# Narrow TensorE products placed between wide ones, and the transposes of the probabilities spread through the work behind them

## The reference

```python
logits = (q @ k) * scale; logits = where(kpos <= qpos, logits, -inf)      # MLA; MoBA adds a bias
p = softmax(logits); out = p @ v
# layer 1
z = (q @ k) * scale
log_1m = where(strict, log_sigmoid(-z), 0.0)
acc = cumsum(log_1m, reverse) - log_1m
w = where(strict, exp(log_sigmoid(z) + acc), 0.0); out = w @ v
```

## Time and profile before

| | us |
|---|---|
| median of 3 runs (lowest to highest) | 1331.95 (1331.87 to 1332.46) |
| the profiled execution | 1332.39 |
| its span | 1330.6 |
| PE busy, share | 1291.9, 97% |
| DVE, ACT, POOL busy | 734.3, 554.5, 260.1 |

### The profile page before, as it was taken

How to read it: one execution, slowest core, us unless ns; L and a number is a source line. 1 busy time by engine, 2 the same in 40 slices (tenths; PEclk the granted TensorE clock), 3 DMA queues, 4 the chain that set the end, 5 groups by cost and what they waited for, 6 DMA issues and landing times.

```text
span 1330.6 us, 17696 instructions
## 1 busy us (share of the span) xinstructions
PE 1291.9 (97%) x6599; PEld 1093.1 (82%) x6599; DVE 734.3 (55%) x998; ACT 554.5 (42%) x885; POOL 260.1 (20%) x205
## 2 busy tenths in 40 slices
PE   6989999999999999999999999999999999999997
PEld 5677788898888888888888888887988888888886
DVE  4777654538644454422288787776574455443223
ACT  5456665546322223322354555454453322223112
POOL 1532200025211111100051111320441111110002
PEclk9989999999999999999999999999999999999999
DMA  5412222122333333333222111311223333332331
GB/s 163 132 43 71 65 72 72 48 79 81 111 95 95 99 101 96 87 101 96 83 79 65 48 48 52 90 48 47 81 81 110 95 95 95 95 112 93 95 96 63
DMA packets 190503, 112.34 MB, mean 84 GB/s; under 512 B 13696, under 2 KB 184773, under 8 KB 190446
## 3 DMA queue, kind: packets, MB, share of 16 engines
q1 hardware_dynamic: 188636, 106.81, 27.6%
q0 software_dynamic: 640, 2.10, 0.5%
q10 hardware_dynamic: 1170, 2.66, 0.5%
HBM read 109.43 MB, written 4.74 MB: 86 GB/s over the span
## 4 chain that ended last, share of the span: by engine, by line
PE 85%; DVE 8%; ACT 3%; issue 2%; POOL 1%; DMA 0%; POOLq 0%; ACTq 0%; SPq 0%; DVEq 0%
PE banks L433 26%; PE banks L435 25%; PE banks L434 25%; PE banks L1712 3%; DVE w_lo L428 1%; PE banks L1742 1%; PE banks L1630 1%; PE banks L1459 1%; DVE logits L1421 1%; PE banks L482 1%; DVE tf L702 1%; ACT logits L1432 1%; DVE probsT_lo L1471 1%; POOL stick_lo L1729 0%; DVE u_lo L712 0%
## 5 line engine op out<-in xcount | busy, mean ns | idle before, releaser
L428 DVE TENSOR_TENSOR w_lo<-w_raw,w_hi 128x1024 fp32r<-128x1024 f32 (+3 forms) x200 | 288.0, 1443 | 264.9 <-ACT w_hi L421 264.7
L433 PE MATMUL banks<-u_hi,w_hi 128*128 128x512 f32 (+1 forms) x1112 | 424.9, 382 | 5.8 <-DVE w_lo L428 4.3
L435 PE MATMUL banks<-u_hi,w_lo 128*128 128x512 f32 (+1 forms) x1112 | 419.1, 377 | 0.0
L434 PE MATMUL banks<-u_lo,w_hi 128*128 128x512 f32 (+1 forms) x1112 | 418.9, 377 | 0.0
L421 ACT ACTIVATE w_hi<-w_raw 128x1024 fp32r<-128x1024 f32 (+3 forms) x200 | 206.0, 1031 | 277.0 <-PE banks L435 277.0
L433 PEld LDWEIGHTS banks<-u_hi,w_hi 128*128 128x128 f32 x1112 | 210.2, 189 | 45.7 <-issue 4.9
L435 PEld LDWEIGHTS banks<-u_hi,w_lo 128*128 128x128 f32 x1112 | 210.1, 189 | 38.8
L434 PEld LDWEIGHTS banks<-u_lo,w_hi 128*128 128x128 f32 x1112 | 210.3, 189 | 37.8 <-issue 1.0
L905 POOL TENSOR_TENSOR up<-up,gate 128x512 f32<-128x512 f32 x44 | 71.8, 1632 | 375.2 <-DVE up L931 358.4
L886 ACT ACTIVATE gate<-gate 128x512 f32<-128x512 f32 x44 | 27.8, 632 | 202.3 <-DVE gate L927 202.3
L1729 POOL TENSOR_TENSOR stick_lo<-softplus,stick_hi 128x1280 fp32r<-128x1280 f32 x14 | 44.1, 3164 | 156.9 <-DVE stick_hi L1725 156.9
(11 more groups left out here) (256 smaller groups left out, 1987.5 us busy)
## 6 DMA issues: line engine op xcount, KB each, us to landing
w_raw<-in_ffn_w_gate_up_dram SPq DMA_DIRECT2D x88, 512.0 KB, 3.6
w_raw<-in_ffn_w_down_dram SPq DMA_DIRECT2D x30, 512.0 KB, 3.6
w_raw<-in_sb_w_qkv_dram SPq DMA_DIRECT2D x24, 512.0 KB, 3.6
w_raw<-in_ab_w_in_dram SPq DMA_DIRECT2D x17, 512.0 KB, 3.6
w_raw<-in_ffn_w_down_dram SPq DMA_DIRECT2D x16, 448.0 KB, 3.6
w_raw<-in_ab_w_out_dram SPq DMA_DIRECT2D x8, 512.0 KB, 3.8
w_raw<-in_sb_w_out_dram SPq DMA_DIRECT2D x8, 512.0 KB, 4.5
bias_by_distance<-bias_rows ACTq DMA_DIRECT2D x1, 2560.0 KB
```

What stands on the lines that cost most here:

```text
L428: dve.tensor_tensor(wl[:, c.slot, 0:w], raw[:, c.slot, 0:w], wh[:, c.slot, 0:w].bitcast(F32), ALU.subtract).then_inc(w_lo, 1)
L433: nc.tensor.matmul(o, lh, rh, start=start, stop=False, skip_group_check=True)
L434: nc.tensor.matmul(o, lh, rl, start=False, stop=False, skip_group_check=True)
L435: return nc.tensor.matmul(o, ll, rh, start=False, stop=stop, skip_group_check=True)
```

## The change

1. `mm3` takes a generator `narrow` and pulls one matmul from it after each of its three; `project`, `item_pe` and `scores_pe` hand it through (the four transposes of a "vt" slot don't use it).
2. `probs_pe` becomes such a generator. A step issues the first transpose, and the other nine go one by one behind the matmuls of slot a where that is a projection, then behind those of the first two score tiles of head `hh + 2`; what is left follows the scores.
3. `scores_pe`: the narrow tile's three matmuls go between those of the 384-wide tile. `values`: the last block's three go between those of the first. `c_pe`: the eight narrow ones go singly behind wide ones. `sb_pv_pe`: the two narrow ones go between and behind the two 512-wide ones. `z_pair_pe`: for each of three terms the two heads' 256-wide blocks, then their two narrow ones (before: six narrow ones in a row, then six 256-wide ones).
4. A tensor of 128 bytes a partition is put ahead of the latent tensors, which moves them by that much.

```diff
+            sb(at0, "latent_line_pad", [P, 32])
...
-        def mm3(o, lh, ll, rh, rl, start, stop):
+        def mm3(o, lh, ll, rh, rl, start, stop, narrow=iter(())):
             nc.tensor.matmul(o, lh, rh, start=start, stop=False, skip_group_check=True)
+            next(narrow, None)
             nc.tensor.matmul(o, lh, rl, start=False, stop=False, skip_group_check=True)
+            next(narrow, None)
-            return nc.tensor.matmul(o, ll, rh, start=False, stop=stop, skip_group_check=True)
+            mm = nc.tensor.matmul(o, ll, rh, start=False, stop=stop, skip_group_check=True)
+            next(narrow, None)
+            return mm
...
-            for i in (3, 1, 2, 0):
+            def first_tile():
+                o = SC[:, ROW_AT[0]:ROW_AT[0] + P]
+                for lq, rk in ((qh, kh), (qh, kl), (ql, kh)):
+                    mm = nc.tensor.matmul(o, lq[:, 0:P], rk[:, 0:P], start=False, stop=lq is ql, skip_group_check=True)
+                    if lq is ql:
+                        mm.then_inc(sc_done, 1)
+                    yield
+
+            for i in (3, 1, 2):
                 mm = mm3(SC[:, at:at + w], qh[:, q], ql[:, q], kh[:, 0:w], kl[:, 0:w],
-                         start=(i != 0), stop=True)
+                         start=True, stop=True, narrow=first_tile() if i == 2 else narrow)
...
-            mm.then_inc(pt_done, 1)
+                    if j == TT - 1:
+                        mm.then_inc(pt_done, 1)
+                    yield
...
+            def last_block():
+                o, at = out_bank[:, P * (TT - 1):T], COL_AT[TT - 1] + at0
+                for lv, rx in ((v[0], xh), (v[0], xl), (v[1], xh)):
+                    nc.tensor.matmul(o, lv[:, buf, TT - 1, cols], rx[:, at:at + P], start=False, stop=False,
+                                     skip_group_check=True)
+                    yield
...
-            for j in (0, 1, 3, 2):
+            for blocks in ((0,), (1,), (2, 3)):
                 for n, (lhs, rhs) in enumerate(Z_TERMS):
-                    for e in range(2):
-                        z_block(par, e, j, lhs, rhs, j != 3 and n == 0)
+                    for j in blocks:
+                        for e in range(2):
+                            z_block(par, e, j, lhs, rhs, j != 3 and n == 0)
...
+            def last_blocks():
+                for j in range(TT):
+                    for n in (nsh, nsl):
+                        yield block(j, TT - 1, n)
+            narrow = last_blocks()
+            for j in range(TT - 1):
+                for jj in range(j, TT - 1):
+                    for n in (nsh, nsl):
+                        mm = block(j, jj, n)
+                        if (j, jj) != (0, 0) and (j, jj, n) != (TT - 2, TT - 2, nsl):
+                            next(narrow, None)
...
-            for j in range(TT):
+            for j, n in ((0, 0), (3, 0), (0, 1), (3, 1), (1, 0), (1, 1), (2, 0), (2, 1)):
...
-                probs_pe(pe, hh)
-                item_pe(pe, a)
+                transposes = probs_pe(pe, hh)
+                next(transposes)
+                if hh % 2 == 0:
+                    item_pe(pe, a, transposes)
+                else:
+                    item_pe(pe, a, transposes)
                 if hh + 2 < NH0:
-                    scores_pe(pe, hh + 2)
+                    scores_pe(pe, hh + 2, transposes)
+                for _ in transposes:
+                    pass
```

More of the change, by code:

```diff
@@ L445, in project @@
                 last = mm3(o, wh[:, c.slot, s], wl[:, c.slot, s], xh[:, first + k, :], xl[:, first + k, :],
-                           start=(first + k == 0), stop=(first + k == total - 1))
+                           start=(first + k == 0), stop=(first + k == total - 1), narrow=narrow)
                 if inside and k == (kt // 2 - 1 if inside_at is None else inside_at):
@@ L1191, in head_of, with item_pe @@
             return 2 * it[1] + it[2]
-        def item_pe(pe, it):
+        def item_pe(pe, it, narrow=iter(())):
             if it is None:
@@ L1211, in item_pe @@
                 m = P if e else MLA_QH
-                mm = project(pe, b[0:m, :], c, KQ, 2 * MLA_QH, e * HD, m, cqh, cql)
+                mm = project(pe, b[0:m, :], c, KQ, 2 * MLA_QH, e * HD, m, cqh, cql, narrow=narrow)
             elif kind == "mk":
-                mm = project(pe, b, c, KKV, P, 0, P, ckh, ckl)
+                mm = project(pe, b, c, KKV, P, 0, P, ckh, ckl, narrow=narrow)
             elif kind == "mv":
-                mm = project(pe, b, c, KKV, P, KKV * P, P, ckh, ckl)
+                mm = project(pe, b, c, KKV, P, KKV * P, P, ckh, ckl, narrow=narrow)
             elif kind == "vt":
@@ L1220, in item_pe @@
             else:
-                mm = project(pe, b, c, KD, P, 0, P, uh, ul)
+                mm = project(pe, b, c, KD, P, 0, P, uh, ul, narrow=narrow)
             mm.then_inc(w_used if last else pj_mm, 1)
@@ L1377, in bass_hybrid_two_layers, with scores_pe @@
                 lo_order[it[:3]] = len(lo_order)
-        def scores_pe(pe, hh):
+        def scores_pe(pe, hh, narrow=iter(())):
             p, e = hh // 2, hh % 2
@@ L1474, in values @@
         def values(out_bank, v, buf, e, xh, xl, at0):
-            for j in range(TT):
-                w, at, cols = T - P * j, COL_AT[j] + at0, slice(HD * e, HD * e + P)
+            cols = slice(HD * e, HD * e + P)
+            def last_block():
[5 more added lines that the diff above has]
+            for j in range(TT - 1):
+                w, at = T - P * j, COL_AT[j] + at0
                 mm = mm3(out_bank[:, P * j:T], v[0][:, buf, j, cols], v[1][:, buf, j, cols],
-                         xh[:, at:at + w], xl[:, at:at + w], start=(e == 0 and j == 0), stop=(e == 1 and j == TT - 1))
+                         xh[:, at:at + w], xl[:, at:at + w], start=(e == 0 and j == 0), stop=(e == 1 and j == TT - 2),
+                         narrow=last_block() if j == 0 else iter(()))
             return mm
@@ L1706, in c_pe, with block @@
             Z = ZB[e]
[L1707 to L1710, removed]
-                    for n in (nsh, nsl):
-                        mm = nc.tensor.matmul(Z[:, at:at + w], lt[:, :], n[:, e, COL_AT[jj]:COL_AT[jj] + w],
-                                              start=False, stop=False, skip_group_check=True)
+            def block(j, jj, n):
+                at, w = COL_AT[j] + (jj - j) * P, T - P * jj
+                return nc.tensor.matmul(Z[:, at:at + w], (negtri if jj == j else negones)[:, :],
+                                        n[:, e, COL_AT[jj]:COL_AT[jj] + w], start=False, stop=False,
+                                        skip_group_check=True)
+            def last_blocks():
+                for j in range(TT):
+                    for n in (nsh, nsl):
+                        yield block(j, TT - 1, n)
+            narrow = last_blocks()
+            for j in range(TT - 1):
+                for jj in range(j, TT - 1):
[3 more added lines that the diff above has]
+                            next(narrow, None)
             mm.then_inc(c_done, 1)
@@ L1738, in sb_pv_pe @@
                 pe.wait_ge(so_read, p * 2 + 1)
-            for j in range(TT):
+            for j, n in ((0, 0), (3, 0), (0, 1), (3, 1), (1, 0), (1, 1), (2, 0), (2, 1)):
                 w, at = T - P * j, COL_AT[j]
[L1741 to L1744, removed]
+                mm = nc.tensor.matmul(bank(b)[:, P * j:T], sv[:, par, e, j, :], (swh, swl)[n][:, e, at:at + w],
+                                      start=(j == 0 and n == 0), stop=(j == 2 and n == 1), skip_group_check=True)
             mm.then_inc(sv_done, 1)
```

2 lines of the change are left out of this document (1 added, 1 removed).

## The result

The changed kernel took 1359.26 us (median of 4 runs, 1356.68 to 1362.00), the kernel before 1332.20 in the same comparison: a ratio of 1.0203 [1.0187, 1.0219]. It is slower by 27 us; forecast were 18. The 1359 lie above the range of the prediction (to 1357). Four more executions of the same kernel later gave 1355.41 (1348.33 to 1358.83), a ratio of 1.0153 [1.0116, 1.0190]. That spread is itself part of the answer.

What follows compares the result with a forecast made beforehand. TensorE's pace through its queue was taken as the bound, except where neighbours hold it up. Terms 2.4 + 4.4 + 1.8 + 9.6 = 18.2 us over the kernel before gave 1350.1, predicted 1350; 8-in-10 range 1337 to 1357.

Steps and rivals of the forecast that it cites:

- Bound and narrow orders: Whole kernel bound by TensorE's queue; reordered narrow matmuls in `c_pe`, `sb_pv_pe`, `values`, narrow score tile, `z_pair_pe` change by 0.
- Rivals A and B: A: loads made further ahead, lone narrow matmuls cost their stream, 1334.4 (chance 0.10); B: also across row changes, 1323.7 (0.05).
- Step 5 and step 12: Nine transposes no longer cover the wait for VectorE's bank read, TensorE full there: net 0.85 and 0.93 us.
- Steps 1, 3: Late transposes delay `probs_act`, then VectorE and the scaling slot c waits for: +2.2 us each.
- Step 0: Late transposes make `probs_act` 2.4 us late, with ScalarE's and VectorE's queues in series behind it: +2.4.
- Rival D: Steps 0, 1 and 3: hidden slack on ScalarE absorbs the late transposes, 1343.3 us; chance 0.07.
- Steps 2, 4: Nine pairs in slot a end before the scores' wait for VectorE, covered by 0.45 us: 0.
- Even MoBA steps: Steps 6, 8, 10: late transposes cost 0; bound of 0.2 us in each of four odd steps.
- Changes of rows: Single transposes among 64-row scores, steps 7, 9, 11, 13: gaps of 2.4 us a step, 9.6 in all.
- rival C: TensorE idles 0.8 to 1 us more in several places of steps 0 to 4, lowering the clock; chance 0.12.
- the lower clock in places where it was full: Sign listed as showing the forecast wrong, pointing to the clock rival (C).

Runs made afterwards that it cites:

- the kernel with the narrow orders alone: Changed kernel with all ten transpositions of a step issued at once as before, new narrow orders and pad kept: 1333.31 us, ratio 1.0004.
- the second profile with four singles: Repeat of the changed kernel with only four transpositions singly among the 64-row scores of steps 7, 9, 11, 13: 1352.53 us, ratio 1.0153 (first 1352.55).
- the second profile: The changed kernel run again unaltered, profiled a second time: 1355.41 us, ratio 1.0153 against the kernel before.
- the four profiles of the table: Changed kernel twice (1359.26, 1355.41 us); kernel before with only the transpositions spread (1355.10); changed kernel with none among 64-row scores (1342.69).
- alone: Kernel before with only the transpositions spread as in the change, no new narrow orders, no pad: 1355.10 us, ratio 1.0170; again 1356.71, ratio 1.0161.
- the run with gaps and no change of rows: Changed kernel with MoBA scores over 128 rows and TensorE waiting for its own matmul ten times in steps 7, 9, 11, 13: 1359.29 us, ratio 1.0205.

## Why the prediction was wrong

- **Bound and narrow orders**: right, lone narrow ones change nothing (1.0004). In the profile of before a load is recorded at the start of the matmul ahead of its own (168.19 and 168.19 with 512-wide ones 0.23 apart, 827.65 and 827.65 in `c_pe`), or with a narrow pair 0.05 behind it, with 0.11 from load to load (827.19 for 827.14, 827.30 for 827.25). None of these stands earlier. Rivals A and B are out. What a load or a narrow matmul takes by itself no trace shows: these loads are recorded 0.19 long and stand 0.11 apart, and the prediction's 0.06 is the distance of two recorded starts (827.08, 827.14). Measured is that a lone narrow one and the 384-wide one behind it take 0.29 together (832.14 to 832.43).
- **Step 5 and step 12**: 1.01 and 1.09 for 0.85 and 0.93. Right; 0.1 of each stands in the kernel with the narrow orders alone too.
- **Steps 1, 3**: 2.32 and 2.21 for 2.2 each, with `probs_act` later by 2.24 in step 3. Right.
- **Step 0**: 2.32 for 2.4, by luck. The 2.4 took the lower clock to last up to 85.4, and no run shows the term as it was worked out. The profile after had full clock there, and there the spreading costs 1.57; the other 0.75 is also in kernels that don't spread in step 0. Where the clock stood at 0.50 up to 87.5 or later, the step was 3.85 to 4.09 longer; in the second profile with four singles (0.50 from 83.0 to 88.3) a product with its transposition took 0.64 there (83.96, 84.60, 85.24). Rival D is out.
- **Steps 2, 4**: 0. Right. **Even MoBA steps**: forecast 0, measured 0.1 each. Where an odd step's scores don't cover it, they also delay VectorE by 0.3 in the next, over the bound of 0.2 that the prediction gave.
- **Changes of rows**: right, twelve in each odd MoBA step, and both directions cost. 0.17 each instead of 0.20, 8.1 instead of 9.6 at full clock. The first load of the other kind begins with its own matmul, and the later the longer the matmul ahead of it is recorded: 0.43 behind the start of a 512-wide one of 0.50 (180.13 to 180.56), 0.32 behind one of 0.39 (168.42 to 168.74 in the profile of before), 0.25 behind a transposition of 0.33 (180.56 to 180.81), 0.40 behind one of 0.47 at the clock of 0.50 (183.73 to 184.13). With the scores over 128 rows the transposition's load stands at 184.33, 0.10 behind the start of the product ahead of it (184.23), and the pair takes 0.34 instead of 0.69.
- **The step that failed** is the one in that same term that left TensorE at full clock. The text took rival C, the clock, only for steps 0 to 4, where TensorE idles, and gave steps 5 to 15 none of it, since they read as busy for 110 of 110 us. In the four odd MoBA steps it fell for 6.8, 6.8, 6.8 and 3.4 us and cost 18.9 - 8.1 = 10.8 in the profiled execution. Without it the steps make 28.1 - 10.8 = 17.3 for the forecast 18.2, and 1349.21 and 1348.33 are the fastest runs with the transpositions spread as in the change, at a clock of 0.992 and 0.991. The prediction's own sign for this was "the lower clock in places where it was full", and that is what came; the forecast's sum had no term for it.
- **Rival C**, the clock in steps 0 to 4, has no part in the first profile (its last fall ahead of step 5 ended at 77.6, before step 0 began at 81.0). It came in other executions: in the second profile steps 0 and 1 took 2.6 more than in the first, with 0.50 from 100.1 on. In eight of eleven profiles a fall began between 98 and 103 us, around the start of step 1; steps 2 and 4 show none in the four profiles of the table (0.01 us or less from before).

The forecast held a warning. By it the scores with their transpositions take 5.3 us, 2.4 of them gaps, and the clock stood low in a stretch where TensorE had gaps too, 1.4 us of 10, though those rows don't show what had lowered it. What stays open is what decides for one execution: the same kernel fell in four of four steps once and in two of four the next time, and alone in none and then two. The one fall in the run with gaps and no change of rows (step 9, 0.50 for 3.4 us) points to the short gaps.

## What to carry to other kernels

Keep matmuls over 64 rows together, and matmuls over 128 rows together. A single one of the other kind costs two changes, 0.34 us here; a group of six has only two changes as well, and cost no more than none (0.3 to 0.4 a step either way). When a change adds many such gaps to a dense stretch, price the clock too, however busy TensorE reads, and give the result a spread instead of a number: nine of the seventeen steps with twelve changes, in five profiles, fell to half speed, for up to 3.1 us each. Before moving work that another engine waits for (here `probs_act`) behind more work, follow that engine's queue to the next wait of TensorE: steps 1 and 3 paid 2.2 to 2.3 each for it and step 0 paid 1.6 at full clock.

## What the runs showed of the hardware

- From a 64-row product of 512 columns to a 128-row transposition 0.43 us (180.13 to 180.56) where 0.23 is usual (168.19 to 168.42), and back 0.26 (to 180.82) where 0.11 is (ten transpositions take 1.28, the last one's record 0.27: 1.01 for nine), by the starts.
- The clock fell with TensorE recorded as busy throughout (6.70 of 6.70 us, and the 4.00 us ahead of it), because the gap is covered in the record by the modelled end of the matmul before it (180.13 + 0.50 lies behind the next start, 180.56). The weight path shows it: busy 2.23 of those 4.00 us.
- Contracting all MoBA scores over 128 rows saves 0.33 to 0.36 in each of eight heads of the kernel before: 0.9977 [0.9968, 0.9987]. A right version would need the other head's rows of the queries at zero, in buffers of their own; it wasn't built.
